# Gated MLP: nine of eleven up-projection iterations as seven block products each

## The reference

```python
def conv_ffn(x, norm_g, w_up, conv_w, conv_b, w_down):
    h = rms_norm(x, norm_g)
    a, b = jnp.split(h @ w_up, 2, axis=-1)
    a = conv(a, conv_w) + conv_b      # causal, 3 taps, each channel by itself
    return (silu(a) * b) @ w_down
```

## Time and profile before

| | |
|---|---|
| median of 3 runs | 1625.05 us (1625.04 to 1625.46) |
| profiled execution, span from first to last instruction | 1624.1 us (the page gives no time beside its span) |
| TensorE busy | 1617.6 us, 7482 matmuls |
| VectorE, ScalarE, GpSimd busy | 971.4, 670.6, 109.9 us |
| DMA | 154.59 MB, mean 95 GB/s |

### The profile page before, as it was taken

How to read it: one execution, slowest core, us unless ns; L and a number is a source line. 1 busy time by engine, 2 the same in 40 slices (tenths; PEclk the granted TensorE clock), 3 DMA queues, 4 the chain that set the end, 5 groups by cost and what they waited for, 6 DMA issues and landing times.

```text
span 1624.1 us, 19782 instructions
## 1 busy us (share of the span) xinstructions
PE 1617.6 (100%) x7482; PEld 1348.9 (83%) x7482; DVE 971.4 (60%) x1167; ACT 670.6 (41%) x807; POOL 109.9 (7%) x157
## 2 busy tenths in 40 slices
PE   9999999999999999999999999999999999999998
PEld 7888888888888888888888888888888888888887
DVE  7267875775666666533362778657756666556222
ACT  5244335532345445522233543345333554454213
POOL 4000000000310000002020000000004000000020
PEclk9999999999999999999999999999999999999999
DMA  5332222223232323323233322222233322232322
GB/s 189 104 117 78 78 78 91 79 68 101 91 99 95 97 97 92 102 92 102 91 116 96 112 78 78 78 91 76 77 94 99 96 93 101 91 103 90 111 91 91
DMA packets 44701, 154.59 MB, mean 95 GB/s; under 512 B 4960, under 2 KB 5472, under 8 KB 44640
## 3 DMA queue, kind: packets, MB, share of 16 engines
q1 hardware_dynamic: 42480, 148.86, 28.0%
q10 hardware_dynamic: 2160, 4.86, 1.1%
HBM read 149.50 MB, written 2.10 MB: 93 GB/s over the span
## 4 chain that ended last, share of the span: by engine, by line
PE 99%; DMA 0%; DVE 0%; ACT 0%; issue 0%; SPq 0%; DVEq 0%; ACTq 0%
PE ps L1045 30%; PE ps L1043 30%; PE ps L1044 30%; PE ps L1051 2%; PE ps L1050 2%; PE ps L1049 2%; PE ps L1172 1%; PE ps L1161 1%; PE ps L1139 1%; PE ps L1143 1%; PE ps L1295 0%; PE ps L1183 0%; DMA xs<-xt 0%; PE ps L1109 0%; PE ps L1180 0%; PE ps L1340 0%
## 5 line engine op out<-in xcount | busy, mean ns | idle before, releaser
L1043 PE MATMUL ps<-u_hi,w_hi 128*128 128x512 f32 x1344 | 525.5, 391 | 0.0
L682 DVE TENSOR_TENSOR w_lo<-w_raw,w_hi 128x1024 fp32r<-128x1024 f32 x274 | 350.6, 1289 | 291.8 <-ACT w_hi L431 287.7
L1045 PE MATMUL ps<-u_hi,w_lo 128*128 128x512 f32 x1344 | 523.3, 389 | 0.0
L1044 PE MATMUL ps<-u_lo,w_hi 128*128 128x512 f32 x1344 | 523.2, 389 | 0.0
L431 ACT ACTIVATE w_hi<-w_raw 128x1024 fp32r<-128x1024 f32 x274 | 286.6, 1055 | 278.7 <-DMA w_raw<-wts 272.0
L1045 PEld LDWEIGHTS ps<-u_hi,w_lo 128*128 128x128 f32 x1344 | 252.3, 188 | 53.0
L1044 PEld LDWEIGHTS ps<-u_lo,w_hi 128*128 128x128 f32 x1344 | 252.5, 188 | 50.9
L1043 PEld LDWEIGHTS ps<-u_hi,w_hi 128*128 128x128 f32 x1344 | 252.5, 188 | 50.5
L1045 PE MATMUL ps<-g_hi,w_lo 128*128 128x512 f32 x264 | 102.7, 389 | 0.0
L1043 PE MATMUL ps<-g_hi,w_hi 128*128 128x512 f32 x264 | 102.7, 389 | 0.0
L1044 PE MATMUL ps<-g_lo,w_hi 128*128 128x512 f32 x264 | 102.7, 389 | 0.0
(11 more groups left out here) (211 smaller groups left out, 2190.1 us busy)
## 6 DMA issues: line engine op xcount, KB each, us to landing
w_raw<-wts SPq DMA_DIRECT2D x274, 512.0 KB, 3.5
q<-q ACTq DMA_DIRECT2D x8, 256.0 KB, 3.5
xs<-xt SPq DMA_DIRECT2D x7, 256.0 KB, 6.6
out<-rows SPq DMA_DIRECT2D x7, 256.0 KB, 2.5
dec<-decay ACTq DMA_DIRECT2D x2, 514.0 KB, 4.1
w_raw<-wts SPq DMA_DIRECT2D x4, 256.0 KB, 6.2
cs<-rope ACTq DMA_DIRECT2D x2, 512.0 KB, 3.6
lastg<-last ACTq DMA_DIRECT2D x1, 256.0 KB, 4.3
```

The source lines that it names most:

```text
L682: nc.vector.tensor_tensor(w_lo[:, s, :], w_raw[:, s, :], w_hi[:, s, :].bitcast(F32), ALU.subtract).then_inc(s_lo, 1)
L1043: nc.tensor.matmul(dst, a_hi, b_hi, start=start, stop=False)
L1044: nc.tensor.matmul(dst, a_hi, b_lo, start=False, stop=False)
L1045: return nc.tensor.matmul(dst, a_lo, b_hi, start=False, stop=stop)
```

## The change

The first two up-projection iterations (PLAIN=2) stay as they are. The other nine (SPLIT=9) are done as 2x2 block products. The weights of an iteration are four quarters: rows 0-511 and 512-1023 of the input channels by the a and the b features (W11, W21, W12, W22). The operand has four quarters too: the two halves of the channels by the first and last 256 tokens. Instead of eight quarter products seven are made, of sums and differences of quarters; each is 24 matmuls of 256 columns (`product`). Four weight parts are sums: W11+W12 and W12+W22 are made by a DMA from GpSimd's queue that adds the second quarter to the tile (`add_parts`, k=1 and 4), W11+W12+W22 and the sum of all four by VectorE (`third_sum`, `fourth_sum`). Here k counts the products from 0 in code; the prediction counts them from 1. Results are combined by copies of partial sums out of PSUM (ScalarE) and subtractions (VectorE), in two halves of the tokens.

The norm goes into the operand: ScalarE multiplies x by the gain in the first plain iteration (`with_gain`, 16 copies of 128x256), GpSimd multiplies by rinv and makes the sums (`combine`, 8 operations of 128x1024), and ScalarE and VectorE make the seven high and low parts in the second plain iteration (`comb_high`, `comb_low`).

The product with b moves to GpSimd for the nine (`gated`). Its high and low parts move into the down-projection for all, two tiles at once (`gated_high`, `gated_low`). The loops over g become straight code, and SP's loop over the ring is cut around the nine iterations. A quarter's slot is reloaded after the product that used it. In the down-projection TensorE's wait for s_gl is unchanged.

```diff
+PLAIN = 2
+PAIRS = FT // 2
+SPLIT = PAIRS - PLAIN
+DOWN0 = UP0 + 4 * PLAIN
 SLABS = DOWN0 + FT
+W11, W21, W12, W22 = range(4)
 
 WO_TILE = 2 * (IN_UNITS + 8)
 UP_TILE = WO_TILE + 8
...
+            def load_split(l):
+
+                base = l * SLABS + DOWN0 - RING + SLOT_CREDIT
+                sp.wait_ge(s_free, base + 1)
+                load_part(l, 0, 0, W11, s_el[0])
+                sp.wait_ge(s_free, base + 2)
+                load_part(l, 0, 1, W11, s_el[1])
+                sp.wait_ge(s_free, base + 3)
+                load_part(l, 0, 2, W22, s_el[2])
+                load_part(l, 0, 6, W21, s_el6[0])
+                sp.wait_ge(s_free, base + 4)
+                load_part(l, 0, 3, W21, s_el[3])
+                load_part(l, 0, 4, W12, s_el[4])
+                load_part(l, 0, 5, W22, s_el[5])
+                for n in range(SPLIT):
+                    done = 7 * (l * SPLIT + n)
+                    more = n + 1 < SPLIT
+                    if more:
+                        if n > 0:
+                            sp.wait_ge(s_prod, done)
+                        load_part(l, n + 1, 6, W21, s_el6[(n + 1) % 2])
+                    sp.wait_ge(s_prod, done + 1)
+                    if more:
...
+            def combine(l):
+
+                a11, s1, s5, a12, s3, s4, a22 = comb
+                early = rinv[:, 0:S // 2].rearrange("p (a t) -> p a t", a=1).broadcast_to([P, 4, S // 2])
+                late = rinv[:, S // 2:S].rearrange("p (a t) -> p a t", a=1).broadcast_to([P, 4, S // 2])
+                pool.wait_ge(s_r, l * 3 + 3)
+                pool.wait_ge(s_xgain, l * 16 + 16)
+                nc.gpsimd.tensor_tensor(a22[:], a22[:], late, ALU.mult).then_inc(s_v, 1)
+                nc.gpsimd.tensor_tensor(late2[:], late2[:], late, ALU.mult).then_inc(s_v, 1)
+                nc.gpsimd.tensor_tensor(a11[:], a11[:], early, ALU.mult).then_inc(s_v, 1)
+                nc.gpsimd.tensor_tensor(a12[:], a12[:], early, ALU.mult).then_inc(s_v, 1)
+                pool.wait_ge(s_v, l * 4 + 4)
+                nc.gpsimd.tensor_tensor(s1[:], a22[:], late2[:], ALU.subtract).then_inc(s_comb, 1)
+                nc.gpsimd.tensor_tensor(s3[:], late2[:], a11[:], ALU.subtract).then_inc(s_comb, 1)
+                pool.wait_ge(s_comb, l * 4 + 1)
+                nc.gpsimd.tensor_tensor(s5[:], s1[:], a11[:], ALU.add).then_inc(s_comb, 1)
+                pool.wait_ge(s_comb, l * 4 + 3)
+                nc.gpsimd.tensor_tensor(s4[:], s5[:], a12[:], ALU.subtract).then_inc(s_comb, 1)
+
+            def add_parts(l, n, k):
+
+                landed, added, which = (s_el[1], s_sum1, W12) if k == 1 else (s_el[4], s_sum3, W22)
+                pool.wait_ge(landed, 16 * (l * SPLIT + n + 1))
+                nc.gpsimd.dma_start(part_raw(l, n, k), wts[DEPTH * SLABS + (l * SPLIT + n) * 4 + which, :, :],
+                                    accum_op=ALU.add).then_inc(added, 16)
+
+            def gated(l, n):
+
+                for h in range(2):
+                    f = 2 * (PLAIN + n) + h
+                    pool.wait_ge(s_c2, l * FT + f + 1)
+                    pool.wait_ge(s_c22, l * SPLIT + n + 1)
+                    pool.wait_ge(s_tile, top_right(l, n))
+                    nc.gpsimd.tensor_tensor(g_raw[:, f, :], cc[:, h, :], cb[:, h, :], ALU.mult).then_inc(s_gf, 1)
...
+                combine(l)
+                add_parts(l, 0, 1)
+                add_parts(l, 0, 4)
+                for n in range(SPLIT):
+                    if n + 1 < SPLIT:
+                        add_parts(l, n + 1, 1)
+                    if n > 0:
+                        gated(l, n - 1)
+                    if n + 1 < SPLIT:
+                        add_parts(l, n + 1, 4)
+                gated(l, SPLIT - 1)
...
+            def with_gain(l, k):
+
+                for q in (k, 4 + k):
+                    for first, tile in ((0, comb[0] if q < 4 else comb[3]), (S // 2, late2 if q < 4 else comb[6])):
+                        nc.scalar.activation(tile[:, k, :], x[:, q, first:first + S // 2], ACT.Copy,
+                                             scale=pcol(l, PAR_FFN + q)).then_inc(s_xgain, 1)
+
+            def comb_high(l, k):
+
+                if k in (0, 3, 6):
+                    act.wait_ge(s_v, l * 4 + 4)
+                else:
+                    act.wait_ge(s_comb, l * 4 + (1, 3, 2, 4)[(1, 2, 4, 5).index(k)])
+                if k in (0, 6):
+                    nc.scalar.activation(comb_hi[k][:], comb[k][:], ACT.Copy, scale=-1.0).then_inc(s_combh, 1)
+                else:
+                    nc.scalar.activation(comb_hi[k][:], comb[k][:], ACT.Copy).then_inc(s_combh, 1)
...
+            def gated_high(l, c):
+
+                act.wait_ge(s_gf, l * FT + 2 * c + 2)
+                last = 7 * SPLIT * (l + 1)
+                act.wait_ge(s_prod, last - 6 if c < 2 else last)
+                nc.scalar.activation(g_hi[:, 2 * c:2 * c + 2, :], g_raw[:, 2 * c:2 * c + 2, :], ACT.Copy).then_inc(s_ghh, 1)
...
-                with act.Fori(0, FT // 2) as g:
+                for g in range(PLAIN):
...
+                        i = UP0 + 4 * g + j
+                        if i + AHEAD < DOWN0:
+                            split_hi(l, i + AHEAD)
+                        elif i + AHEAD > DOWN0:
+                            part_high(l, 0, i + AHEAD - DOWN0 - 1)
+                        if g == 0:
+                            with_gain(l, j)
+                        if j == 1:
+                            plain_tap(l, g, 0)
+                            silu(l, 2 * g)
+                        if g == PLAIN - 1 and j > 0:
+                            for k in ((0, 1), (2, 3), (4, 5, 6))[j - 1]:
+                                comb_high(l, k)
+                        if j == 3 and g + 1 < PLAIN:
+                            plain_tap(l, g, 1)
+                            silu(l, 2 * g + 1)
...
                 for i in range(DOWN0, SLABS):
+                    if i == DOWN0:
+                        last_quarter(l, SPLIT - 1)
+                        act.wait_ge(s_prod, 7 * (l + 1) * SPLIT)
+                        split_hi(l, DOWN0 + 2)
+                        for h in range(2):
+                            tap(l, SPLIT - 1, h)
                     if i + AHEAD < SLABS:
                         split_hi(l, i + AHEAD)
+                    if i - DOWN0 + 1 < PAIRS:
+                        gated_high(l, i - DOWN0 + 1)
+                    if i == DOWN0:
+                        for h in range(2):
...
+            def comb_low(l, k):
+
+                dve.wait_ge(s_combh, l * 7 + k + 1)
+                if k in (0, 6):
+                    dve.wait_ge(s_comb, l * 4 + 4)
+                    nc.vector.scalar_tensor_tensor(out=comb_lo[k][:], in0=comb[k][:], scalar=-1.0, in1=comb_hi[k][:].bitcast(F32),
+                                                   op0=ALU.mult, op1=ALU.subtract).then_inc(s_combl, 1)
+                else:
+                    dve.wait_ge(s_comb, l * 4 + 4)
+                    nc.vector.tensor_tensor(comb_lo[k][:], comb[k][:], comb_hi[k][:].bitcast(F32), ALU.subtract).then_inc(s_combl, 1)
+
+            def part_low(l, n, k):
+
+                m = l * SPLIT + n
+                dve.wait_ge(s_eh, 7 * m + k + 1)
+                if k == 1:
+                    dve.wait_ge(s_sum2, m + 1)
+                if k == 2:
+                    dve.wait_ge(s_sum4, m + 1)
+                nc.vector.tensor_tensor(part_lo(l, n, k), part_raw(l, n, k), part_hi(l, k).bitcast(F32), ALU.subtract).then_inc(s_elo, 1)
+
+            def third_sum(l, n):
+
+                m = l * SPLIT + n
+                dve.wait_ge(s_sum1, 16 * (m + 1))
+                dve.wait_ge(s_el[2], 16 * (m + 1))
+                nc.vector.tensor_tensor(part_raw(l, n, 2), part_raw(l, n, 2), part_raw(l, n, 1), ALU.add).then_inc(s_sum2, 1)
+
+            def fourth_sum(l, n):
+
+                m = l * SPLIT + n
+                dve.wait_ge(s_sum2, m + 1)
+                dve.wait_ge(s_el6[n % 2], 16 * (l * ((SPLIT + 1 - n % 2) // 2) + n // 2 + 1))
+                nc.vector.tensor_tensor(part_raw(l, n, 6), part_raw(l, n, 6), part_raw(l, n, 2), ALU.add).then_inc(s_sum4, 1)
...
+            def gated_low(l, c):
+
+                dve.wait_ge(s_ghh, l * PAIRS + c + 1)
+                nc.vector.tensor_tensor(g_lo[:, 2 * c:2 * c + 2, :], g_raw[:, 2 * c:2 * c + 2, :], g_hi[:, 2 * c:2 * c + 2, :].bitcast(F32),
+                                        ALU.subtract).then_inc(s_gl, 2)
...
+                        i = UP0 + 4 * g + j
+                        if i + AHEAD < DOWN0:
+                            split_lo(l, i + AHEAD)
+                        elif i + AHEAD == DOWN0 + 1:
+                            part_low(l, 0, 0)
+                        elif i + AHEAD == DOWN0 + 2:
+                            third_sum(l, 0)
+                            fourth_sum(l, 0)
+                            part_low(l, 0, 1)
+                        if j == 1:
+                            plain_out(l, g, 0)
```

(86 more changed lines are left out.)

285 lines of the change are left out of this document (226 added, 59 removed).

## The result

The changed kernel takes 1675.99 us (median of 4 runs, 1674.52 to 1676.56), the one before 1625.05 beside it: a ratio of 1.0311 [1.0297, 1.0326]. The forecast was 1684, in a range of 1655 to 1709.

What follows compares the result with a forecast made beforehand. TensorE was taken as the bound, on the path for 99% of the span. Per layer -14.4+22.4+19.7+1.8 = +29.5; 1624.1+59.0 = 1683.1, plus 0.95 between span and median gives 1684 us, range 1655 to 1709.

Steps and rivals of the forecast that it cites:

- both waits: Forecast case: TensorE waits before the first product and in the down-projection's first half; 1684 us, chance 0.73.
- loss 2: Down-projection: gated low parts queue behind a slab's split, slabs 1 to 10 each 1.97 us late; 19.7 us per layer.
- loss 1: Before the first product: TensorE waits for operand parts behind GpSimd's eight operations and VectorE's row; 22.4 us per layer.
- the slow start: First matmuls after a long TensorE wait run slower; 1.8 us added per long wait, bounds 0 and 1.8.
- the steady iterations: Block iterations in steady state: other engines' work is hidden behind TensorE's products; cost 0.
- gaps inside the eighteen iterations: Sign of a wrong forecast: TensorE gaps within product iterations, which were to take 20.2 us each without gaps.
- The gain: Up-projection: seven products of 24 shorter matmuls at 0.120 us save 1.60 us per iteration, 28.8 us over eighteen.
- nearly 2 us of room everywhere: Block iterations: VectorE and ScalarE finish their parts nearly 2 us before TensorE wants them, so cost 0.
- the 9.2 where they would have decided: Block iterations: an adding DMA may take 9.2 us before TensorE waits for the sum it delays.
- rival (c): Block iterations: adding DMA takes over 9.2 us, making every iteration late; near 1733 us at 12 us, chance 0.07.
- the equal sharing: Before the first product: GpSimd and VectorE each lose what the other uses, adding 5.6 us to GpSimd's end.
- That slab's slot is free when slab s-2 ends, that is when slab s-1 starts: Down-projection: counts the chain from a slab's start, 7.41 us to the gated low part against a slab of 5.44.

Runs made afterwards that it cites:

- g: f with the gated products of the nine iterations also moved from GpSimd to VectorE; 1626.03 us, ratio 1.0011 to the kernel before.
- h: g with ScalarE's two SiLUs of token tiles 2 and 3 behind copy_u in the first block iteration; 1626.54 us, ratio 1.0007.
- i: h with operand 4 (W12+W22) of the first block iteration summed by VectorE instead of the adding DMA; 1612.33 us, ratio 0.9932.
- d: The changed kernel with the changes of run a, b and c together; 1636.44 us, ratio 1.0081 to the kernel before.
- f: d with GpSimd's eight operations on VectorE, gated parts two slabs ahead, convolutions of tiles 2 and 3 in the first block iteration; 1630.33 us, ratio 1.0034.
- b: The changed kernel with half of ScalarE's sixteen gain copies before its root, the rest in the first step behind it; 1668.3 us, ratio 1.0276.
- c: The changed kernel with the last plain evacuation ahead of the third weight sum and three low parts moved into the first block iteration; 1659.01 us, ratio 1.0209.
- run a: The changed kernel with gated_high and gated_low ahead of the weight slab's split in the down-projection; 1655.2 us, ratio 1.0191.
- run e: The changed kernel plus 224 small TensorE matmuls per layer into an unused bank, filling the wait before the first product; 1685.25 us, ratio 1.0365.

## Why the prediction was right, and where its terms were off

The case was the forecast one, both waits, and time and range held. The mechanism was right too: TensorE stood idle where it was said to, for the engines that were named. The sizes were not, and their errors partly cancel (in layer 0 loss 2 was forecast 6.9 us and loss 1 2.3 us too long, the slow start and the steady iterations together 3.2 us too short). One of the signs of being wrong came true as well, gaps inside the eighteen iterations. By its steps, in layer 0:

**The gain** held: the product matmuls start 0.12 us apart at full clock, as the earlier trace rows had it. Over the whole iterations it is 0.1193; that makes the gain 30.9 us instead of 28.8, and what the next step lost larger by the same. I keep 0.120, so that the terms compare with the forecast. The trace shows 186.4 us for nine iterations (514.89 to the first down-projection matmul at 701.25) against 9 x 20.16 = 181.4, and the 5 us between are the next step and the slow start.

**The steady iteration**, taken at 0 with "nearly 2 us of room everywhere", cost 2.3: 186.4 less 181.4 less the slow start of 2.7. The two main kinds of wait inside it are the rows `copy_u` and `cb L1412` above, 4.6 us in the kernel, none over 1.0. What makes ScalarE's copy and VectorE's evacuation late in some iterations and not in others stays open; g shows that GpSimd's products are not the main cause. The adding DMAs took 7.7 us, under the 9.2 where they would have decided; rival (c) didn't come. In the first iteration of the layer, though, where there is no product to hide behind, such a DMA became the bound once the longer waits were gone, and taking it out was worth 11 to 14 us in the two layers (h against i). My step followed the steady state alone.

**Loss 1**, forecast 22.4, was 20.1 (20.29 less 0.23). Two errors cancel in part. GpSimd ended 3.6 us earlier than worked out. Of this 1.1 is its earlier start, and 2.5 come from the interference, which isn't the equal sharing that I took from the earlier trace rows: most of GpSimd's operations went from 2.39 to about 2.84 (one to 3.31), while VectorE's waited for their end (0.75 became 2.77, 1.23 became 3.41), and those that read PSUM stayed at 0.68. Against that, VectorE's row took 16.0 instead of 15.3: 14.1 of work and the stall of 1.87 for the adding DMA. TensorE also came to the wait 0.6 earlier than forecast. The Trainium skill (SBUF — State Buffer, section "SBUF: two separate sides") calls the pair of ports between the two an exclusive lock and not a split of bandwidth, held for a whole instruction, against a VectorE operation with two SBUF inputs; d against f agrees, 2.74 against 1.23 for the same split. Runs b and c confirm the rest of the chain: each piece taken out of it shortened the wait, by 7 us (b) and 9 us (c) per layer.

**Loss 2**, forecast 19.7, was 12.8: slab 0 starts at 701.25 and the slab eleven later at 773.89, 72.64 us for 11 x 5.44 = 59.84. The step that failed is "That slab's slot is free when slab s-2 ends, that is when slab s-1 starts". Without waits the two are one moment; once TensorE waits they aren't. The chain counts from the end, so a slab's wait shortens the next one's by its own length, and of the ten slabs only six wait by more than 1 us. The chain itself was nearly right: 3.9 of load (714.4 to 718.29), and 7.4 until the low part stands at 721.75, for 7.41. Half of ten times 1.97 would have been 9.9. The first wait costs 2.2, as the chain gives with its load at 4.1. The second costs 2.9, since ScalarE's split and high part stand behind the last pair's SiLUs there, which wait for VectorE's convolution, as in run a. Run a shows the cause, 21.7 to 5.2.

**The slow start**, forecast 1.8, was 2.7 (28 matmuls in 6.0 us instead of 3.3). The trace now shows the granted clock at 0.50, which it didn't at the kernel's start; run e shows that the idle time is what lowers it.

The sum with these: -14.4 + 20.1 + 12.8 + 2.7 + 2.3 = +23.5 in layer 0. Of the +49.6 of the trace that leaves 26.1 for layer 1. There the same steps are -14.4 + 20.0 + 14.4 + 6.0 = +26.0: loss 1 as long, loss 2 longer (74.3 us from the first down-projection matmul at 1530.17 to the end of slab 10, less 59.84), and 6.0 for slow start and steady iterations together. The later waits of the down-projection are 1.7 to 2.0 us there instead of 1.2 to 1.5, and behind the wait that ends at 1545.65 the granted clock was 0.50 from 1546 to 1548. Net, a layer lost 24.8 us where 29.5 were forecast; most of the difference is loss 2.

## What to carry to other kernels

When a wait is forecast in a loop, write the recurrence from the event that really releases the resource (an end) and put the wait itself in: here it took a third off the loss. A helper engine that does two-input work beside VectorE cost VectorE nearly the helper's whole instruction here, so eight such operations can be cheaper on VectorE itself. And look at the first pass of a pipelined loop by itself: its loads have nothing to hide behind, and there a transfer that adds (7.7 us) was worth replacing by a 1.2 us sum. In the other iterations the forecast point of 9.2 us wasn't reached; replacing it there was not tried.

## What the runs showed of the hardware

A VectorE operation with two SBUF inputs that met one of GpSimd's ended 0.55 us (one of 0.75) to 1.08 us (one of 1.23) after GpSimd's two-input operation ended; GpSimd's own went from 2.39 to between 2.68 and 3.31 in the changed kernel. An operation of VectorE that reads PSUM stayed at 0.68.

A DMA that adds 512 KB to a tile took 7.5 to 7.7 us from issue to landing in the changed kernel (medians, 6.4 to 7.8 over all runs), beside plain loads at 3.4 to 5.0. By the page's part 3 the adding queue moved 18.88 MB in 6.6% of the sixteen engines' span, 5.9 us of all sixteen engines per MB, against 3.0 for queue q1 with the loads.

TensorE's granted clock fell to 0.50 in the long idle time and was back at 1.00 only after about 6 us of work. Waits of 1.2 to 2.6 us in the down-projection left it at 1.00 in layer 0 of the changed kernel, while three waits of 1.8 to 1.9 us in run e were followed by 0.64 to 0.79. In the first block iteration of run h it was still 1.00 after a wait of 2.4 us and 0.50 after one of 4.2; in i it stayed at 1.00 after one of 3.0.
